# Moving the score products ahead of the value products in every step of three attention loops

## The reference

```
for l in range(DEPTH):                       # DEPTH = 2
    h = rms_norm(xp, ln_mix[l])
    qa, ka, va, la, qb, kb, vb = project_heads(h, w_in[l], b_f[l])
    o = concatenate([fox_prompt(qa, ka, va, la),          # 8 heads x 64, causal, with decay
                     swa_prompt(qb, kb, vb, sinks)])      # 8 heads x 64, window of 2+1 chunks, sinks
    xp = xp + o @ w_out[l]
    xp = xp + cross_attend(rms_norm(xp, ln_mem[l]), ...)  # 4 heads x 128, into 256 memory tokens
    xp = xp + conv_ffn(rms_norm(xp, ln_ffn[l]), ...)      # width 2816
```

## Time and profile before

| | us |
|---|---|
| time, median of 3 runs | 3662.96 (3658.25 to 3667.80) |
| the profiled execution's own time | 3667.80 |
| its span | 3666.0 |
| PE busy | 3391.6 (93%) |
| DVE busy | 1948.3 (53%) |
| POOL busy | 1201.7 (33%) |
| ACT busy | 860.2 (23%) |

### The profile page before, as it was taken

One profiled execution on the slowest core, in us unless ns is written; L12 is line 12 of the kernel. 1 busy time (PEld: TensorE's weight loads), 2 busy tenths in 40 slices (PEclk: granted clock), 3 DMA queues, 4 the chain that ended last, 5 costly groups with the idle time before them and its releaser, 6 DMA issues. The chain is left out here.

```text
span 3666.0 us, 52968 instructions
## 1 busy us (share of the span) xinstructions
PE 3391.6 (93%) x21112; PEld 3258.7 (89%) x21112; DVE 1948.3 (53%) x3592; ACT 860.2 (23%) x2008; POOL 1201.7 (33%) x976
## 2 busy tenths in 40 slices
PE   6998997888999999999989999978988999999997
PEld 6988887778889999999988888877888999999997
DVE  5554444877664444444554444548767543444345
ACT  4331231444320000000232322224433100000001
POOL 4113112333243343333441122124233433333331
PEclk9999998999999999999989999988999999999998
DMA  4111112111011111111121112111111111111111
GB/s 144 42 46 53 42 37 62 55 38 44 27 41 44 44 45 46 41 44 47 41 72 42 49 41 59 44 46 58 43 36 30 41 44 44 44 46 42 47 44 63
DMA packets 85255, 175.53 MB, mean 48 GB/s; under 512 B 10401, under 2 KB 13601, under 8 KB 84609
## 3 DMA queue, kind: packets, MB, share of 16 engines
q1 hardware_dynamic: 72112, 133.03, 12.8%
q10 hardware_dynamic: 12896, 38.97, 3.5%
HBM read 150.23 MB, written 16.29 MB: 45 GB/s over the span
## 5 line engine op out<-in xcount | busy, mean ns | idle before, releaser
L599 POOL TENSOR_TENSOR WH<-RAW,zero 128x512 fp32r<-128x512 f32 x484 | 545.5, 1127 | 2378.8 <-PE PS L619 2366.6
L619 PE MATMUL PS<-HH,WH 128*128 128x384 f32 (+1 forms) x3312 | 873.5, 336 | 101.9 <-POOL WL L601 19.4
L619 PE MATMUL PS<-HL,WH 128*128 128x384 f32 (+1 forms) x3312 | 855.9, 331 | 0.0
L619 PE MATMUL PS<-HH,WL 128*128 128x384 f32 (+1 forms) x3312 | 854.2, 330 | 0.0
L619 PEld LDWEIGHTS PS<-HH,WH 128*128 128x128 f32 x3312 | 593.9, 191 | 124.0 <-POOL WL L601 22.4
L601 POOL TENSOR_TENSOR WL<-RAW,WH 128x512 fp32r<-128x512 f32 x484 | 660.8, 1365 | 37.9
L619 PEld LDWEIGHTS PS<-HL,WH 128*128 128x128 f32 x3312 | 597.0, 191 | 0.0
L619 PEld LDWEIGHTS PS<-HH,WL 128*128 128x128 f32 x3312 | 594.7, 190 | 0.0
L1675 DVE TENSOR_TENSOR XT<-PS,XT 128x320 f32<-128x320 f32 x448 | 303.3, 718 | 269.6 <-PE PS L619 269.4
L619 PE MATMUL PS<-G0H,WH 128*128 128x384 f32 (+1 forms) x960 | 287.6, 348 | 44.9 <-DVE XT L1526 29.1
L1108 ACT ACTIVATE PTH<-PS 128x512 fp32r<-128x512 f32 (+4 forms) x320 | 165.5, 520 | 682.1 <-PE PS L619 680.9
(11 more groups left out here) (249 smaller groups left out, 5191.7 us busy)
## 6 DMA issues: line engine op xcount, KB each, us to landing
RAW<-in_slabs SPq DMA_DIRECT2D x484, 256.0 KB, 2.7
XR<-decays ACTq DMA_DIRECT2D x16, 512.0 KB, 5.7
XT<-in_xT SPq DMA_DIRECT2D x8, 544.0 KB, 7.9
XR<-decays ACTq DMA_DIRECT2D x16, 272.0 KB, 6.7
out_fk<-T ACTq DMA_DIRECT2D x8, 544.0 KB, 2.7
out_fv<-T ACTq DMA_DIRECT2D x8, 544.0 KB, 2.8
out_y<-YT ACTq DMA_DIRECT2D x8, 544.0 KB, 3.2
RX<-ST ACTq DMA_DIRECT2D x16, 136.0 KB, 2.4
```

The lines of the kernel that those rows point to most:

```text
L599: pool.tensor_tensor(WH[:, s, :], RAW[:, s, :], zero[:, 0:1].to_broadcast([128, HALF]), ALU.add).then_inc(w_hi, 1)
L619: ins = pe.matmul(*a, **k)
```

## The change: order of a step on TensorE, the table of parts and the order of one drain

In TensorE's step the scores of s+1 now stand behind gap 0, and the values product of s-3 behind gap 1: transposes, gap 0, scores, gap 1, values, gap 2. On VectorE the drain of a part that ended in gap 1 now stands ahead of the low half of the values product, instead of behind it. ScalarE's, GpSimd's and SyncE's orders stay as they are. In the table, a step -1 (which has no values product) may now use gaps 1 and 2, which both lie behind its scores; swa's first output projection puts two parts in step -1 instead of one, two in each of the steps 0 to 10, and none in step 11.

```
-                fill |= {-1: spread(v[:1], (2,)), 0: ...}
+                fill |= {-1: spread(v[:1], (1, 2)), 0: ...}
...
-            fill = {-1: spread(fox[:1], (2,)), 11: spread(fox[-1:], (0, 1, 2))}
-            fill |= {s: spread(fox[2 * s + 1:2 * s + 3], (0, 1, 2)) for s in range(11)}
+            fill = {s: spread(fox[2 * s + 2:2 * s + 4], (1, 2) if s < 0 else (0, 1, 2)) for s in range(-1, 11)}
...
                     parts(pe, fill, s, 0)
-                    if s >= 3:
-                        values(pe, steps[s - 3], s - 3, rings[s - 3])
-                    parts(pe, fill, s, 1)
                     if s + 1 < len(steps):
                         ...
                         scores(pe, steps[s + 1])
+                    parts(pe, fill, s, 1)
+                    if s >= 3:
+                        values(pe, steps[s - 3], s - 3, rings[s - 3])
                     parts(pe, fill, s, 2)
...
+                    parts_out(s, 1)
                     if s >= 3:
                         high, low = steps[s - 3]["rows"]
                         lo(dve, [...]).then_inc(o_free, 1)
-                    parts_out(s, 1)
```

More of the change, by code:

```diff
@@ L425, in fox_fill @@
                 v = tile_parts(("v", pair), "T32")
-                fill |= {-1: spread(v[:1], (2,)), 0: spread(v[1:2], (0, 1, 2)), 1: spread(v[2:], (0, 1, 2))}
+                fill |= {-1: spread(v[:1], (1, 2)), 0: spread(v[1:2], (0, 1, 2)), 1: spread(v[2:], (0, 1, 2))}
             return fill
```

## The result

The changed kernel takes 3753.65 us (median of four runs, 3746.72 to 3758.52), the kernel before 3665.26 in the same comparison: a ratio of 1.025, 95% interval 1.0232 to 1.0268, so 92 us slower by the ratio and 88 by the medians. The prediction said 3730 (3695 to 3772) and slower. The profiled execution took 3758.27 us with a span of 3756.5, 90.5 more than before. What follows compares the two profiled executions. "Interval" means the time from TensorE's transposes in one step to those in the next, and it has the number of the first of the two; the first transposes of an attention stand in its step 2.

The account below looks back on a forecast made before the run. It took a loop between TensorE and VectorE to bound swa and mem, and TensorE fox. Terms sum to 33.5 us a layer, +67 for two, on 3667.8: 3734.8, given as 3730 (3695 to 3772) since that execution lay above the median.

Parts of the forecast that it names:

- the loop: Swa and mem: next part A waits for values product, HL, reduction and drain in turn; two-part step 6.12 against 4.97 us.
- Term 1: Swa steps with two parts: +1.15 us each, +1.39 where a hook precedes the reduction; 17.3 us a layer.
- its own case: Whole kernel: the main forecast of lengthened steps, 3730 us, with its own range 3705 to 3752; weight 0.72.
- clock rival: Lengthened swa and mem steps: more idling drops TensorE's clock in every second of 62 steps, +34, 3764 us; chance 0.15.
- Term 2: Swa steps 25 to 28 with three parts: 6.71 us against 5.70, +1.0 each, 4.0 us a layer.
- Term 3: Swa memory-part steps: +0.9 in five, +1.73 in steps 13 and 22, 0 in steps 17 to 20; 8.0 us a layer.
- Term 4: Mem steps 13 to 18 with three parts: +0.64 each, 3.8 us a layer; steps with projection parts 0.
- Term 6: Gains at the start of swa, steps 0 to 2 about 0.6 each, and step 11 worth 0.4: together -2.2 us.
- Term 5: Fox pairs: steps 2 to 11 cost 0, step 12 costs 0.65, step 13 nothing net; 2.6 us a layer.
- the prediction's own sign: Changed profile: the forecast counts as wrong if fox grows by over 1 us a pair.
- one such pair goes and one comes: Fox step 13: one neighbour pair of parts with an exposed drain disappears and one appears, so no net cost.
- +0.1 for each step: Fox: upper end of the zero estimate, for each of 80 steps, from a probabilities buffer freed one scores product later.

Follow-up runs that it names:

- e9: Changed kernel, VectorE's low half of the values product moved behind the next reduction and drain in swa and mem only, except at hooks: 3723.21 us, ratio 1.0165.
- e2: Changed kernel with the old order in the last steps of each attention, where no scores are left to issue: 3744.46 us, ratio 1.0207.
- e10: Changed kernel with the edits of e2, e4, e8 and e9 together, the new order staying in all other steps: 3684.83 us, ratio 1.0052.
- e4: Changed kernel with the old order in the first fox pair of layer 0 alone: 3743.03 us, ratio 1.0224.
- e1: Changed kernel, VectorE's low half of the values product moved behind the next step's reduction and drain in all attentions, fox included: 3742.07 us, ratio 1.0202.
- e3: Changed kernel's new table places, but its new order only in the first three steps of each attention, old order after: 3657.41 us, ratio 0.9977.
- e5: Changed kernel with the old order from step 3 on in all eight fox pairs; swa and mem keep the new order: 3729.63 us, ratio 1.0174.
- e7: e3 with VectorE's low half of the values product behind the next reduction and drain in swa and mem: 3664.96 us, ratio 0.9993.
- e8: Changed kernel with VectorE's third rotary embedding moved from step 4 of swa to step 5: 3745.23 us, ratio 1.0214.

## Why the prediction was right, and where its sizes were off

Right: the sign, and the loop. Term 1's step, 6.12 us from A to A, measured 5.98. Swa as a whole, 27.1 predicted for a layer, took 26.8 and 28.9. VectorE did not pass over the waiting HL, and e9, which takes HL out of that place, brings 31 us. The memory-part step, 6.12 predicted, took 6.10. The XT wait rose to 70.3 us, 80 expected; that total is a weak sign, for in e9, whose steady steps are back, it is still 58.6.

The measured 3753.65 lies 1.7 us above the 3705 to 3752 that the prediction gave its own case, and nearer to the clock rival's 3764 than to 3730. So the time alone does not choose between them. The steps' lengths and e9 do.

Term 1 met its number partly by chance. The interval with the embedding grew by 4.7 and 4.9 us, where the term has 1.39, and 2.5 us of that are the longer operations of the GpSimd collision. "At this point VectorE waits anyhow" was asked for single instructions of VectorE, not for what GpSimd would be doing at the new time.

Term 2, the three-part steps: 1.0 us each predicted, 0.25 to 0.68 measured. Term 3: steps 17 to 20, costed at 0, cost 3.4 us in each layer, because their reduction stands behind HL too, drain or no drain, as e9 shows; the whole group took 10.7 and 4.4. Term 4, mem: -0.1 and 3.9 for 3.8, but the 3.9 is luck. The six steps of the term took 1.3 and 2.3 us more, and 1.5 of layer 1's 3.9 lie in step 7, which is not in it; in layer 0 the first two intervals were 2.3 us shorter. Term 6: -4.2 and -2.4 for -2.2.

Term 5, fox, failed, and makes up the 24 us between 67 and 91. It was 2.6 a layer; 20.1 and 10.5 were measured. By the prediction's own sign, over 1 us a pair, it was wrong there. A pair other than the first of a layer took about 2.7:

- Step 12: 0.65 predicted, 0.93 measured, with a wait of 0.65.
- Step 13 was taken as "one such pair goes and one comes". None went: the values product does not hide the drain, as the rows under e2 show. 0.96 a pair.
- The steps at the start of a pair, costed at nothing: 0.75 a pair, most of it in step 3. By the trace ScalarE's first PTH there starts 5.5 us after the transposes instead of 3.4, as it waits for a buffer that the values product frees later. The end "+0.1 for each step" was the place of this, but the cost sits in one or two steps; the steps 6 to 11 have only 0.04 or 0.05 each, and step 2 gives 0.2 back. No experiment took it alone; it is still there in e10, pair by pair (0.74 to 0.77).
- The first pair of layer 0: 11.7 us in steps 3 to 5, through the memory norm and the clock (e4). The prediction named no hook of fox, and its lower clock was a rival for the lengthened steps of swa and mem only.

The clock rival was half right. In swa of layer 0 it did not come: the many waits of 0.7 to 1.8 us went with a grant of 0.90 against 0.88. In one stretch of layer 1 it did; the kernel before, then the changed one, the same eight steps:

```profile
2469.97:2512.95 42.98, 35.28 (x241) 31.27 (x241) 36.98 (x110) 21.90 (x78) 9.61 (x9) 0.92 0.16 55
```

```profile
2531.95:2585.74 53.79, 40.48 (x235) 35.70 (x234) 34.93 (x109) 23.56 (x80) 9.51 (x8) 0.81 0.10 34
```

The stretch is 10.8 us longer, and the lower clock brings at most 7 of it: a grant of 0.81 means 2 x 0.19 x 53.79 = 20.4 us at 1.2 GHz, against 2 x 0.08 x 42.98 = 6.9 before, and half of such time is lost. Layer 0 grew by 8.6 us over the same steps, so this stretch is only a third of the 6.7 us by which layer 1's two-part steps exceed layer 0's. The Trainium skill, "TensorE: Matmul & The Clock Gate", section "A second HAM failure mode: psum-queue depth-cycling", was weighed in the prediction; of the stretches looked at in swa, the trace agrees with it in this one and not in layer 0's. More of it came in the first fox pair, where TensorE had been busy without a gap and one wait followed. Over the span the mean grant fell from 0.967 to 0.963, at most the 18 us estimated above, of 90.5.

## What to carry to other kernels

An instruction that is issued earlier on one engine gains nothing if its reader still stands, on its own engine, behind something that was issued later: move the two together, or cut the reader loose as e9 did. When a cover is claimed ("the values hide the drain"), follow the drain's own queue, and ask whether what stands ahead of it needs the cover's result. And when a change shifts the phase of two engines by some microseconds, look at what a third one is doing at the new time.

## What the runs showed of the hardware

- A short wait in a stretch in which TensorE has no gap can cost many times its length: 1.38 us, and steps 3 to 5 of the pair 11.7 us longer; 0.39 us, and up to 4.9. But the same 0.39 us at the same place had a drop behind it in only five of e1's eight pairs, and waits of 0.65 us at a pair's end were followed by a grant of 1.00 (e1, 160 to 175 us). What sets them apart is open.
- The clock also drops without any wait that the profile shows: steps 10 and 11 of a pair took 14.69 us in e10 (9.12 and 5.57) instead of 8.64 as in the changed kernel, and the same 6.0 to 6.3 us appear in one or two pairs of the profiles of e3, e5, e7 and e8, always in these two steps.
- The 10 to 20 us by which runs of one kernel differ here are mostly the clock. In 13 executions of the changed kernel the shortest span, 3744.9 us, had a mean grant of 0.965 and the longest, 3762.8, had 0.960; lost time, estimated as one minus the grant times the span, is 131 and 151 us, a difference of 19 for 18 measured. e5's profiled execution, with two such drops, is 12 us above its other three.

Three stretches of e10, of which the middle one is the two long intervals of the second pair:

```profile
245.86:251.77 5.91, 5.91 (x42) 5.06 (x41) 2.70 (x8) 1.83 (x7) 0.00 (x0) 0.95 0.02 4
251.77:266.46 14.69, 14.69 (x66) 13.27 (x66) 6.89 (x17) 5.66 (x14) 0.00 (x0) 0.56 0.00 0
266.46:280.00 13.54, 13.54 (x98) 13.54 (x97) 4.94 (x12) 2.65 (x7) 0.00 (x0) 1.00 0.29 80
```

TensorE is busy for all 14.69 us and granted 0.56.
